# Five reorderings, a buffer of its own for one feed-forward weight tile, and one expert decode in a single piece, in a one-core two-block model kernel

## The reference, cut to what matters

```python
# PEER: 8 heads, 16 experts each, for each of 256 tokens
s = einsum(q, sub_keys); top_s, top_i = top_k(s, 16)        # two lists of 16
cand_s = top_s[0][:, None] + top_s[1][None, :]              # 16 x 16
fin_s, fin_pos = top_k(cand_s, 16)
idx = top_i[0][fin_pos // 16] * 128 + top_i[1][fin_pos % 16]   # the "decode"
out = sum_k softmax(fin_s)[k] * gelu(expert_u[idx[k]] . h) * expert_v[idx[k]]
# layer 0: GLA plus attention over 256 memory rows, then w_out, then
# conv_ffn: (silu(conv3(x @ w_up)[:2816]) * conv3(x @ w_up)[2816:]) @ w_down
# layer 1: NSA (compressed + selected + window) plus memory attention, w_out, conv_ffn
```

## Time and profile before

| | us |
|---|---|
| median of 3 runs (1631.59 to 1637.02) | 1634.73 |
| the profiled execution | 1635.63 |
| its span, first to last instruction | 1633.8 |
| PE busy in it | 1509.1 |
| DVE / ACT / POOL busy | 941.8 / 412.5 / 596.8 |
| mean granted TensorE clock (1 is 2.4 GHz) | 0.982 |

### The profile page before, as it was taken

The page is one execution under the profiler, slowest core; times in us unless marked ns, Lnnn a source line. Parts: engine busy times, 40 slices in busy tenths (PEclk is TensorE's granted clock), DMA queues, the critical chain, the costliest instruction groups (busy, mean ns, idle before and its releaser), DMA issues. The chain is left out here.

```text
span 1633.8 us, 22069 instructions
## 1 busy us (share of the span) xinstructions
PE 1509.1 (92%) x7680; PEld 1137.3 (70%) x7682; DVE 941.8 (58%) x2401; ACT 412.5 (25%) x1006; POOL 596.8 (37%) x525
## 2 busy tenths in 40 slices
PE   7999899898999877777799999999999999999998
PEld 6999845554455323232357778999999878899997
DVE  5652686666766867666556535555552135555554
ACT  2120232222222222222125422111122145311112
POOL 4850243333433444334333006555510000455551
PEclk9999999999999999999999999999997999999999
DMA  8464799999999999999974118544334310555431
GB/s 335 158 225 158 298 427 426 427 426 427 426 409 426 420 426 428 427 421 415 428 288 135 66 63 332 166 155 157 125 120 128 108 48 1 213 173 167 156 128 39
DMA packets 63383, 420.63 MB, mean 257 GB/s; under 512 B 7340, under 2 KB 7788, under 8 KB 16812
## 3 DMA queue, kind: packets, MB, share of 16 engines
q0 software_dynamic: 38560, 277.19, 40.8%
q1 hardware_dynamic: 24736, 142.35, 25.0%
HBM read 417.28 MB, written 3.45 MB: 258 GB/s over the span
## 5 line engine op out<-in xcount | busy, mean ns | idle before, releaser
L2137 PE MATMUL wide<-arena 128*128 128x512 f32 x1024 | 472.1, 608 | 91.4 <-ACT arena L658 91.4
L2137 PEld LDWEIGHTS wide<-arena 128*128 128x128 f32 x1024 | 189.6, 192 | 351.5 <-issue 193.2
L1418 DVE CUSTOM_DVE_ANT_0 arena<-arena,wide 128x1024 f32<-128x1024 f32 x256 | 312.5, 1221 | 184.8 <-DMA arena<-uv_dram,arena 179.1
L498 POOL DMA_INDIRECT arena<-uv_dram,arena x256 | 259.4, 1013 | 403.4 <-PE wide L2137 286.8
L658 ACT ACTIVATE arena<-arena 128x2 f32<-128x2 f32 (+4 forms) x205 | 72.2, 354 | 527.6 <-DVE arena L1418 409.6
L2377 PE MATMUL wide<-arena,wring 128*128 128x256 f32 x704 | 158.6, 379 | 0.0
L1630 DVE SCALAR_TENSOR_TENSOR arena<-arena,prm 128x255 f32<-128x255 f32 (+1 forms) x152 | 126.0, 849 | 55.6 <-ACT arena L658 55.5
L2377 PEld LDWEIGHTS wide<-arena,wring 128*128 128x128 f32 x704 | 131.0, 190 | 16.1
L1664 DVE TENSOR_TENSOR arena<-bank,arena 128x128 f32<-128x128 f32 x266 | 74.0, 290 | 105.1 <-PE bank L2337 101.6
L509 POOL TENSOR_TENSOR arena<-arena 128x512 f32<-128x512 f32 x15 | 20.2, 1348 | 299.0 <-ACT arena L658 298.3
L658 ACT ACTIVATE arena<-bank 128x128 f32<-128x128 f32 (+8 forms) x101 | 40.3, 401 | 311.2 <-PE bank L2337 104.4
(11 more groups left out here) (296 smaller groups left out, 2139.5 us busy)
## 6 DMA issues: line engine op xcount, KB each, us to landing
wring<-ffn_dram SPq DMA_DIRECT2D x44, 1024.0 KB, 5.1
wring<-ffn_dram SPq DMA_DIRECT2D x44, 512.0 KB, 3.5
wring<-win_dram SPq DMA_DIRECT2D x15, 1024.0 KB, 5.3
wring<-wout_dram SPq DMA_DIRECT2D x12, 1024.0 KB, 4.8
wring<-wq_dram SPq DMA_DIRECT2D x5, 1024.0 KB, 7.1
wring<-mix_dram SPq DMA_DIRECT2D x4, 1024.0 KB, 5.5
arena<-uv_dram,arena POOLq DMA_INDIRECT x256, 11.9
wring<-memkv_dram SPq DMA_DIRECT2D x4, 1024.0 KB, 9.1
```

The source lines that it names most:

```text
L498: pool.indirect_dma_start(out=G[:, n % NBUF, :], out_offset=None, in_=a["uv"], in_offset=bass.IndirectOffsetOnAxis(ap=idx[:, u, r:r + 1], ...
L1418: V.tensor_tensor_reduce(out=G[:, n % NBUF, 0:D], in0=G[:, n % NBUF, 0:D], in1=wide[:, 0:2, :].rearrange("p a b -> p (a b)"), scale=1.0, s ...
L2137: ins = MM(wide[:, 2 + h, :], diag[:, n % 4, e, :], G[:, r % NBUF, D + 512 * h:D + 512 * (h + 1)], start=r % (HEADS * TOPK) == 0, stop=r % ...
```

## The change

1. `ffn1` up tile 0 gets its own place, `front1`, in the buffer `kvx`, whose last reader is the group `cmp_hid` early in layer 1. It leaves the ring: `ffn1` tile j (from 1) now takes ring slot j - 1 behind `wout1`, so all later tiles move up by one slot.
2. Unit 0 of PEER is selected and decoded like all others, in 13 steps; POOL waits once for all 16 indices.
3. `finish(hT)` after PEER is split: tiles 0 and 1, then the two query pieces and the scaling of `gla_qk0`, then tiles 2 to 7.
4. GLA: `probs(1)` moves in front of `decayed(3)`, `probs(2)` in front of `keep_pairs(4)`, `probs(3)` in front of `keep_pairs(5)`.
5. `wout0`: group by group, all eight terms of each.
6. NSA: `nsa_probs(0)` in front of `nsa_max(2)`.

```diff
-          ("wout1", 4, 2048), ("ffn1", FT, 3072)]
+          ("wout1", 4, 2048), ("ffn1", FT - 1, 3072)]
...
-            USED.append(("group", GROUP0[_name] + _s + 1) if _s < PLAIN else ("prod", 7 * (_s - PLAIN + 1) + 7 * SEVEN * layer))
+            j = _s + layer
+            USED.append(("group", GROUP0[_name] + j + 1) if j < PLAIN else ("prod", 7 * (j - PLAIN + 1) + 7 * SEVEN * layer))
...
+        front1 = kvx.rearrange("p a k t -> p (a k t)")[:, 0:2048]
...
                 if name in ("ffn0", "ffn1"):
                     layer = int(name == "ffn1")
+                    n0, slots = n0 - layer, FT
 
                     def load_up(s):
+                        if layer and s == 0:
+                            sp.wait_ge(group_full, GROUP0["cmp_hid"] + 1)
+                            sp.dma_start(front1, a[name][0][:, 0:2048]).then_inc(front1_in, 16)
+                            return
...
             def gather(u):
-                pool.wait_ge(idx_ready, u + 2 if u else 1)
+                pool.wait_ge(idx_ready, u + 1)
                 pool.sem_inc(fence["pool"])
                 for r in range(TOPK):
                     n = u * TOPK + r
-                    if n == TOPK // 2:
-                        pool.wait_ge(idx_ready, 2)
-                        pool.sem_inc(fence["pool"])
...
-            def finish(dst, src, col):
-
-                for k in range(KT):
+            def finish(dst, src, col, ks=range(KT)):
+
+                for k in ks:
...
-            select_in_halves()
+            for step in range(13):
+                select(0, step)
             finish_half(T0, range(4, 8), normed)
...
-            finish(hT, xT, fin[:, 2, :])
+            finish(hT, xT, fin[:, 2, :], range(0, 2))
             b = full("gla_qk0")
             for m in range(2):
                 V.scalar_tensor_tensor(out=gq[32 * m:32 * m + 32, 3, :], in0=b[DK:128, m * S:(m + 1) * S], scalar=float(DK) ** -0.5,
                                        in1=rstd[DK:128, :], op0=ALU.mult, op1=ALU.mult)
             V.tensor_tensor(halves(b, DK), halves(b, DK), rstd[0:DK, :].unsqueeze(1).broadcast_to([DK, 2, S]), ALU.mult).then_inc(scaled0, 1)
+            finish(hT, xT, fin[:, 2, :], range(2, KT))
             norm("mean_fin", xT, [(xT, "g_final", 0)])
...
             probs(0)
+            probs(1)
             decayed(3)
             maxi(2)
             keep_pairs(3)
-            probs(1)
             decayed(4)
             maxi(3)
+            probs(2)
             keep_pairs(4)
-            probs(2)
             decayed(5)
+            probs(3)
             keep_pairs(5)
-            probs(3)
...
-            for J in range(3):
-                nsa_max(J)
+            nsa_max(0)
+            nsa_max(1)
             nsa_probs(0)
+            nsa_max(2)
...
-            for n in range(4):
-                for i in range(4):
+            for i in range(4):
+                for n in range(KT):
                     wout0(i, n)
-            for i in range(4):
-                for n in range(4, KT):
-                    wout0(i, n)
...
                 def up(j, mean=None):
                     b = begin(stage, j)
-                    w = slot(stage, j)
+                    if layer and j == 0:
+                        pe.wait_ge(front1_in, 16)
+                    w = front1 if layer and j == 0 else slot(stage, j - layer)
```

More of the change, by code:

```diff
@@ L365, in program @@
         qk_kept = sem("qk_whole_heads_kept")
+        front1_in = sem("ffn1_front_in")
         onehot_in, bias_dram = sem("onehot_in"), sem("bias_dram")
@@ L514, in weight_sums @@
             def weight_sums(layer, n):
-                r = SLOT0[f"ffn{layer}"] + PLAIN + n
+                r = SLOT0[f"ffn{layer}"] - layer + PLAIN + n
                 w = wring[:, r % RING, :]
@@ L1374, in select @@
                                            op0=ALU.mult, op1=ALU.add).then_inc(idx_ready, 1)
[L1376 to L1407, removed]
-                join()
-                decode(1)
             def weigh(u):
@@ L2306, in wout0 @@
                     done(ins)
-            for n in range(4):
-                for i in range(4):
-                    wout0(i, n)
             for i in range(4):
-                for n in range(4, KT):
+                for n in range(KT):
                     wout0(i, n)
             def ffn(stage, layer, norms, gains, mean):
-                g0, n0, k0 = GROUP0[stage], SLOT0[stage], layer * FT
+                g0, n0, k0 = GROUP0[stage], SLOT0[stage] - layer, layer * FT
                 for n in range(4):
```

## The result

The changed kernel took **1613.27 us** (median of 4 runs, 1610.59 to 1620.45) beside 1633.31 for the kernel before on the same chip: ratio 0.9881, 95% interval 0.9851 to 0.9910. The profiled execution took 1610.59 us, with a span of 1608.7 against 1633.8: 25.1 us less, where the sum had 15.5.

A forecast was written before the change was run, and what follows sets the result against it. DMA was taken to bound the 650 us of gathers, PE and its waits the rest. Terms +2.0 - 5.1 - 1.7 - 2.4 - 4.4 - 3.9 = -15.5 from 1635.63, less 0.9 for the median, gave 1619.2 us; range 1615 to 1627.

The forecast's parts named there:

- the sum: Whole kernel: the six parts' terms added to -15.5 us against the profiled execution of 1635.63 us.
- Decode, +2.0: PEER's start: first gather 2.55 us later, of which 2.0 us of DMA time is lost; DVE's gain worth nothing.
- `finish`, -5.1: Before gla_qk1: PE starts 2.0 us earlier and its 64 records lose 3.1 us of slow clock.
- `probs`, -1.7: GLA: PE's waits of 0.83 and 0.84 us before the transposes of jobs 1 and 3 go.
- `wout0`, -2.4: wout0: PE's wait of 2.39 us for weight tile 3 goes, as it is asked for after 24 pieces.
- NSA, -4.4: NSA: first transpose 1.60 us earlier, 3.1 us of half clock gone, 0.3 us put on ACT's copy.
- `ffn1`, -3.9: ffn1 start: tile wait of 2.21 us and 1.76 us of slow clock go; more hT overlap costs 0.1.
- the clock falls all the same: Rival: clock still falls in GLA and NSA, 1625.4 us, or at one of them, 1622.3; chance 0.25.
- The gathers kept their stock: Rival, PEER: gathers lose their stock of full buffers and DMA idles each turn, up to 1644.8 us; chance 0.02.
- the 424 named as a sign of failure: Gather stage: the prediction fails if DMA drops under 424 GB/s between 182 and 832 us.
- The masks and `g_out`: Rivals: GLA mask load late, 1621.2 us, chance 0.04; g_out late in wout0's group 0, within a 0.04 rival.
- the change does what it says: Opposing rival: g_out or ffn1 tile 1 comes late; both together give back 3 us, 1622.2; chance 0.04.

The follow-up runs named there:

- b_split: Kernel before with nsagl's sixteen light matmuls in two groups of eight, one behind each half of nsamq: median 1624.96 us against 1630.93 in its batch.
- gl_split: Changed kernel with nsagl's sixteen light matmuls in two groups of eight, one behind each half of nsamq: median 1611.49 us.
- s_wout0: gl_split with wout0 put back in the order of before: median 1614.01 us, +2.5 against gl_split.
- before_again: The kernel before, run again unchanged with a second profile: profiled execution 1633.66 us.
- s_ffn1: gl_split with the first tile of the second feed-forward layer back in the ring: median 1612.99 us, +1.5 against gl_split.
- best_both: best_pool with the 32 light matmuls of cmp_s in two groups, one behind each half of keys1(0): median 1607.43 us, ratio 0.9851 to the kernel before.
- s_pool: Changed kernel, nsagl not split, with POOL's hidden sums ahead of its first weight sums in the second feed-forward layer alone: median 1611.36 us.
- gl_twice: Changed kernel with the sixteen light matmuls of nsagl issued twice: median 1625.2 us.
- best_pool: gl_split with unit 0 decoded in halves and POOL's hidden sums ahead of its first weight sums in both feed-forward layers: median 1607.39 us.

## Why the prediction was wrong

**The step that failed is the baseline of the sum**: "All sums are against the profiled execution", with its distance to the median put at 0.9 us. That execution held 17 us at half clock around `cmp_hid`, 7.7 us of time, and the prediction never listed them. They were read as part of the kernel; they are a draw that each execution makes anew. The changed kernel's lower group has its median at 1612.1; with 7.7 us more that is 1619.8, where the upper group lies (1619.7) and where the forecast lies (1619.2). Nine of sixteen didn't draw it, and the median of four or of sixteen lies among those, at 1613.3. The three times shown before the change spread over 5.4 us, and the prediction put that down to noise of some 1.5 us on either side instead of asking what made it.

The sum of the gain itself held: the medians of the two upper groups, 1635.4 and 1619.7, differ by 15.7 us and those of the two lower ones, 1626.4 and 1612.1, by 14.3, where the sum had 15.5. That it comes so close is in part luck, since its terms were off in both directions, as the steps below show.

The medians of all times differ by more, 1631.6 - 1613.3 = 18.3 us. Written by the split of `nsagl`, that is 13.5 between the split kernels, and 6.6 that the split takes from the kernel before, less the 1.8 that it takes from the changed one; this is how the four medians add up and explains nothing by itself. By the mean clocks the fall is about as frequent in both kernels (33 of 76, 7 of 16). What sets the medians apart is that the one of the kernel before lies in its middle group (1629.0 to 1631.9), 4.8 us above its lower one at nearly the same mean clock, and that the changed kernel has no such group. The middle group was never profiled. `b_split` has no times above 1628.4, so the split removes it too, but what makes it and why the edits remove it stays open.

By the steps:

- *Decode, +2.0.* The first gather is 2.1 us later where 2.5 was forecast, and only 1.0 us reaches the end of the stage. From 178 to 190 us DMA moves 321 to 332 GB/s in the eleven profiles with the one piece and 375 to 379 in the six with halves, some 0.6 MB less where the sum had 0.84; what makes up the rest by the end of the stage is not shown. The direction held: the edit costs time.
- *`finish`, -5.1.* -5.0 between the two first profiles, 2.8 when undone. The wait of 1.8 is firm; the 3.1 us of clock were one draw of 3.1, 1.8, 1.7 and 0.1. The mask's load is late as worked out, and harmless: DVE waits for it and starts 0.8 us later than in the earlier trace rows, and PE doesn't wait.
- *`probs`, -1.7.* -2.1 and 1.1: right within what can be told.
- *`wout0`, -2.4.* -4.3 in the two profiles and 2.5 when undone. The fall behind this wait stood in the rows (26.96 us for 116 records is 0.232 each, against 5.34 / 24 = 0.222 at full clock), and the prediction missed it; so it forecast 29.8 us for the run of 128 records, which took 27.79. The median shows less of it than the profiles: the profile of `gl_split` has a fall near 1272 that costs 1.7 us and that of `s_wout0` has none there, so the ground of the comparison draws too.
- *NSA, -4.4.* -4.4 and 4.9: right in mechanism and size, with 0.45 us for ACT's copy where 0.3 was put.
- *`ffn1`, -3.9.* -3.4 in the two profiles, 1.5 when undone. The wait goes, but the 1.8 us of clock behind it came in one of the four profiles that have the wait (24 records in 7.10 us, and in 5.42 in `before_again`, `b_split` and `s_ffn1`). And `hT` cost more in the changed kernel: 6.33 us where the sum had an estimated 0.1 on top of 5.34. The 5.34 itself belonged to the execution with the fall; the other three with the tile in the ring had 6.8 us and a wait of 1.2, so against them the edit saves 1.45 us of wait for the tile (`s_ffn1`) and 0.5 of the wait for `hT`. The Trainium skill's rule on the shared port pair (SBUF — State Buffer, section "SBUF: two separate sides"), by which an operation of DVE with two inputs in SBUF and one of GpSimd that reads SBUF lock each other out, was named in the prediction against this part. The prediction put its price at 1.1 us. The runs agree with the rule: 6.33 us beside POOL, 3.25 without. The wait of PE that it makes is 0.73 us.

**The rival "the clock falls all the same" was aimed wrong.** It asked whether the clock would fall in the edited places of the changed kernel. It didn't, in the profiles of it. The same doubt should have gone to the kernel before: whether its falls are there in every execution. They aren't. The gathers kept their stock: the DMA share from 182 to 832 us is 1.01 as before. The rate is 422 GB/s, which by the letter is under the 424 named as a sign of failure, but by 0.5%, and PEER ends 1.6 us later, not the tens of us of that rival. The masks and `g_out` made PE wait nowhere, and the change does what it says.

## What to carry to other kernels

Before summing, list every stretch at half clock in the profiled execution, also where nothing waits and nothing is edited, and treat each as a draw with a price and a chance; single times that lie in groups, as the two here with nothing between 1613.6 and 1617.5, are a sign that there are such draws. Where light matmuls (few columns) run back to back, as the 36-column ones here, try heavy ones between them: it costs no work, took 6.0 us off the median of the kernel before in one batch, and with both splits the six times of `best_both` agree within 0.4 us. When engine A's writes are on PE's path and engine B's work beside them is not, give B the job that waits for A first, and look at when B's other results are really asked for.

## What the runs showed of the hardware

TensorE's clock fell to 0.50, the 1.2 GHz level, while PE was busy 100% of the time: at the end of 3.7 us of 36-column matmuls (`before_again`) or in the scores right behind them (the first profile of the kernel before, and `s_pool`), inside them where they were doubled (`gl_twice`), and never in the ten profiles where eight matmuls of 256 columns stood between two groups. It didn't fall in the three profiles of the changed kernel either, which has the light matmuls in one piece: so they make the fall possible and not certain. It then stayed at 0.50 through 64 matmuls of 68 columns, which ran in 13.92 instead of 7.82 us, and rose again in the heavy ones behind. Behind one and the same idle of 1.83 us its price was 3.1, 1.8, 1.7 or 0.1 us, from execution to execution. The Trainium skill (TensorE: Matmul & The Clock Gate, Part 1) says of a kernel's first matmuls that the moment at which the clock changes varies from run to run, since what the gate watches isn't aligned with the kernel. The four durations at `gla_qk1` vary in the same way; no run here shows why.

POOL's tensor operations on SBUF beside DVE's two-input operations double the latter's time, 6.33 against 3.25 us for eight in the second feed-forward layer (the changed kernel and `s_pool`), and 6.44 against 3.25 in the first (the changed kernel and `best_pool`).
